# Gathering the experts' tokens with native float32 products from one copy of h

## Chip, core and metric

The kernel runs on one core of one Trainium2 chip. The metric is the device time of one execution in microseconds (us), taken as the median of three runs. TensorE (PE in the profile) does all the matrix products; ScalarE (ACT) and VectorE (DVE) empty its accumulators (PSUM) and compute the small things between; GpSimd (POOL) and SyncE (SP) mostly start transfers.

## What is computed

One inference step of a network with four layers over 256 tokens (128 context tokens and 128 latent tokens, width 1024). Each layer mixes the tokens (pooling, attention, Fourier, pooling) and then applies a mixture of 16 experts, of which each token uses two out of one group of four. All data are float32.

```python
def moe(h, router_w, router_b, w_gate, w_up, w_down):
    scores = jax.nn.sigmoid((h @ router_w).astype(jnp.float32))
    ...
    gates = jnp.sum(jax.nn.one_hot(idx, N_EXPERTS, dtype=jnp.float32) * wts[..., None], axis=-2)
    g = jnp.einsum('bnd,edf->bnef', h, w_gate)
    u = jnp.einsum('bnd,edf->bnef', h, w_up)
    a = jax.nn.silu(g) * u * gates[..., None].astype(h.dtype)
    return jnp.einsum('bnef,efd->bnd', a, w_down)
```

The kernel does not compute every expert for every token. It collects the tokens of an expert into 64 slots, computes the expert for these, and adds the result back to the tokens.

## The kernel before

**Order of the work.** Each engine has one hand-written program, and semaphores tie them together. A layer is a mixer, a norm, the router, and then a loop over the four groups of experts (line 1359 on PE, 664 on ACT, 1009 on DVE). With these inputs each group needs one round of 64 slots per expert, so the loop runs 4 times per layer and 16 times in all.

**Weights.** All weights come through one ring of 12 slots of 1 MiB (`ring`), loaded by SP in the order in which PE uses them. SP starts the load of a unit as soon as PE has used the unit 12 places before it (`s_used`), and PE waits for a unit in `unit` (line 1039). One pass of the expert loop uses 24 units. Behind the experts of layer 0 come 8 units of `ada_w` (used in two halves, with the norm between), then the units of `attn_wqkv`, of which the first product (line 1145) needs two at once. Behind the experts of layer 2 come 8 units of `ada_w` and then one of `pool_w` (line 1099).

**Loads by POOL.** At the first norm of layer 1 POOL starts the loads of `braw` (a table of many short rows), `kattn`, `ck` and `cv` (lines 462 to 465). They are released by `s_ms`, which DVE raises in line 707, so they follow the end of the experts of layer 0.

**The router.** PE computes the logits (line 1282), then turns h so that tokens are on the partitions (`by_token`, line 1289, four pieces of 128x512). ACT copies each piece into `h_hi` with rounding to float32r (`high`, line 634), and DVE writes what the rounding left off into `h_lo` (`low`, line 887). Pieces 2 and 3 reuse the banks of 0 and 1, so PE waits for `s_tlo` before them (line 1298). Meanwhile DVE ranks the experts (lines 893 to 927); its `s_mask` releases PE's counting products (lines 1309 to 1313), but PE first goes through the copies of x into the accumulators (line 1305). From the counts DVE makes the positions (lines 942 to 952) and the first `onehot` (line 997), and this releases the first gather.

**The gather.** It is a matrix product too: h, with tokens on the partitions, is the stationary operand (128x128), and the matrix `onehot` (token to slot, four experts side by side, 256 columns) streams past it. There are 8 blocks of channels and 2 sequences, and each product is done for `h_hi` and for `h_lo`: 32 products of 128x128 by 256 columns in each pass of the loop. ACT copies each pair of blocks from PSUM to `xg` (line 669). Later in the pass DVE makes the next `onehot` (line 997).

**The rest of a pass.** Gate and up projections (lines 1388 and 1390, which run side by side in the two halves of the array), the turn of their result (line 1412), the down projection (line 1425), and the combination (line 1435).

Of the kernel before, what the change touches and what calls it, by code (L numbers as in the profile page):

```python
# [156 lines left out]
def build(nc, x_prompt, x_sample, cache_k, cache_v, c, c_ctx, ada_w, ada_b, norm1_g, norm2_g, pool_w,  # L157
# [4 lines left out]
    with ctx:  # L162
# [57 lines left out]
        with ExitStack() as moe:  # L220
            hT = sb("hT", [P, DB, T], F32, moe)
            junk = sb("junk", [P, NSEQ * D], F32, moe)
            tmp = sb("tmp", [P, 512], F32, moe)
            h_hi = sb("h_hi", [P, NSEQ, D], F32R, moe)
            h_lo = sb("h_lo", [P, NSEQ, D], F32R, moe)
            xg = sb("xg", [P, DB, GROUP, SLOTS], F32, moe)
            onehot = sb("onehot", [P, NSEQ, GROUP, P], F32R, moe)
            gated = sb("gated", [P, NSEQ, GROUP, P], F32, moe)
            gatedT = sb("gatedT", [P, GROUP, T], F32, moe)
            gu = sb("gu", [P, FB, P], F32, moe)  # L230
            sg = sb("sg", [P, FB, SLOTS], F32, moe)
            act = sb("act", [P, FB, SLOTS], F32, moe)
# [96 lines left out]
        s_sig = sem("s_sig")  # L329
        s_tok = sem("s_tok")  # L330
        s_thi = sem("s_thi")
        s_tlo = sem("s_tlo")
        s_mask = sem("s_mask")
        s_pos = sem("s_pos")
        s_posx = sem("s_posx")
# [156 lines left out]
        def _(ac):  # L492
# [133 lines left out]
            def router(l):  # L626
                ac.wait_ge(s_lg, l + 1)
                nc.scalar.activation(r_sc[:, :, :], ps[:, B_Y, 0:2 * E].rearrange("p (s e) -> p s e", s=NSEQ),
                                     ACT.Sigmoid).then_inc(s_sig, 1)

                def high(i):
                    ac.wait_ge(s_tok, 4 * l + i + 1)
                    m = (i % 2) * 64
                    nc.scalar.activation(h_hi[:, i // 2, :].rearrange("p (b m) -> p b m", b=DB)[:, :, m:m + 64],
                                         ps[:, i % 2, :].rearrange("p (m b) -> p b m", b=DB), ACT.Copy).then_inc(s_thi, 1)

                high(0)
                high(1)
                for s in range(NSEQ):
                    ac.wait_ge(s_bc2, 2 * l + s + 1)  # L640
                    nc.scalar.activation(g2x[:, s, :], ps[:, B_ACC + s, :], ACT.Copy).then_inc(s_g2x, 1)
                high(2)
                high(3)
# [42 lines left out]
        def _(v):  # L686
# [192 lines left out]
                ada_mods(9)  # L879
                projected(l, "four", 2, (6, 7, 4, 5))  # L880

            def low(l, i):
                v.wait_ge(s_thi, 4 * l + i + 1)
                m = (i % 2) * 64
                hi = h_hi[:, i // 2, :].rearrange("p (b m) -> p b m", b=DB)[:, :, m:m + 64]
                lo = h_lo[:, i // 2, :].rearrange("p (b m) -> p b m", b=DB)[:, :, m:m + 64]
                v.tensor_tensor(lo, ps[:, i % 2, :].rearrange("p (m b) -> p b m", b=DB), hi.bitcast(F32),
                                ALU.subtract).then_inc(s_tlo, 1)

            def router(l):  # L890
                v.wait_ge(s_sig, l + 1)
                sc = r_sc[:, :, :]
# [23 lines left out]
                    link(v.tensor_tensor(r_ge[:, 0:n, :], r_ge[:, 0:n, :], r_gt[:, 0:n, :], ALU.add))  # L916
                    link(v.tensor_reduce(out, ge, AX_X, ALU.add))

                low(l, 0)
                low(l, 1)  # L920
                best = r_best[:, :]
                rank(best.rearrange("p (s g) -> p s g", s=NSEQ), r_gs[:, :, :], NSEQ)
                link(v.tensor_scalar(best, best, 0.0, None, ALU.is_equal))
# [3 lines left out]
                v.tensor_tensor(mask.rearrange("p s (g e) -> p (s g) e", e=GROUP), r_rank[:, :, :],  # L927
                                best.unsqueeze(2).to_broadcast([P, NSEQ * NG, GROUP]), ALU.mult).then_inc(s_mask, 1)
                v.wait_ge(s_mask, l + 1)
                low(l, 2)  # L930
                low(l, 3)
                link(v.tensor_tensor(r_w[:, :, :], sc, mask, ALU.mult))
                link(v.tensor_reduce(r_den[:, :], r_w[:, :, :], AX_X, ALU.add))
                link(v.reciprocal(r_den[:, :], r_den[:, :]))
# [21 lines left out]
            for l in range(DEPTH):  # L956
                base = bases[l]
                if l == 0:
                    norm_chain(0)
                    ada_rows(0, 0, 0)  # L960
                    ada_mods(0)
                else:
                    out_of_experts(base)
                    norm_chain(2 * l)
                    ada_first = {1: 4, 2: 9, 3: 10}[l]
                modulated(l, 0, 2 * l)
                if l > 0:
                    ada_rows(ada_first, l, base)
                if KINDS[l] == 0:
                    mixer_pool(l)  # L970
                    if l == 0:
                        ada_rows(1, 0, 0)
                        ada_mods(1)
                    else:
                        ada_mods(10)
                    pool_added(l)
                elif KINDS[l] == 1:
                    attention(l)
                else:
                    fourier(l)  # L980
                norm_chain(2 * l + 1)
                if l == 0:
                    ada_rows(2, 0, 0)
                    ada_mods(2)
                if l == 3:
                    ada_rows(11, l, base)
                    ada_mods(11)
                modulated(l, 1, 2 * l + 1)
                router(l)
                if l == 0:  # L990
                    ada_rows(3, 0, 0)
                    ada_mods(3)

                def onehots(group, g, count):
                    pos = posx[:, :, :, :].rearrange("p k s e -> p (k s e)")[:, bass.ds(group * 8, 8)]
                    gate = gx[:, :, :, :].rearrange("p g s e -> p (g s e)")[:, bass.ds(g * 8, 8)]
                    v.tensor_tensor(onehot[:, :, :, :].rearrange("p s e c -> p (s e) c"),  # L997
                                    iota.unsqueeze(1).to_broadcast([P, 8, P]),
                                    pos.unsqueeze(2).to_broadcast([P, 8, P]), ALU.is_equal).then_inc(s_oh, 1)
                    v.wait_ge(s_oh, count)  # L1000
                    v.tensor_tensor(gated[:, :, :, :].rearrange("p s e c -> p (s e) c"),
                                    onehot[:, :, :, :].rearrange("p s e c -> p (s e) c").bitcast(F32),
                                    gate.unsqueeze(2).to_broadcast([P, 8, P]), ALU.mult).then_inc(s_gated, 1)

                v.wait_ge(s_posx, 1)
                onehots(0, 0, base + (l + 1))
                v.wait_ge(s_g2x, 2 * (l + 1))
                n = v.value_load(rounds[0:1, l:l + 1], min_val=1, max_val=MAX_ROUNDS)
                with v.Fori(0, n * NG) as k:
                    it = v.snap(base + k)  # L1010
                    it4 = v.snap(it * 4)
                    g_next = v.snap((k + 1) & (NG - 1))
                    k_next = v.snap(k + 1)
                    v.wait_ge(s_oht, it * 2 + 2)
                    onehots(k_next, g_next, it + (l + 2))
                    for e in range(GROUP):
                        v.wait_ge(s_silu, it4 + (e + 1))
                        v.tensor_tensor(act[:, :, :], sg[:, :, :],  # L1018
                                        ps[:, B_T, :].rearrange("p (j c) -> p j c", c=P)[:, :, SLOTS:2 * SLOTS],
                                        ALU.mult).then_inc(s_prod, 1)  # L1020
                        v.wait_ge(s_used, used(EXPERTS_AT[l] + AT_IN_GROUP[("dn", e, 1)], l, it))
                        for s in range(NSEQ):
                            ins = v.tensor_tensor(ysb[:, e % 2, s, :], ps[:, B_Y, :], g2x[:, s, :], ALU.mult)  # L1023
                        ins.then_inc(s_y, 1)
                bases.append(v.snap(base + n * NG))
# [12 lines left out]
        def _(pe):  # L1038
# [237 lines left out]
            def router(l, base):  # L1276
# [18 lines left out]
                if l == 0:  # L1295
                    ada(3, 0, 4, l, base)
                for i in (2, 3):
                    pe.wait_ge(s_tlo, 4 * l + i - 1)
                    by_token(i)


# [22 lines left out]
            for l in range(DEPTH):  # L1324
# [29 lines left out]
                router(l, base)  # L1354

                pe.wait_ge(s_rounds, l + 1)
                pe.wait_ge(s_tlo, 4 * l + 4)
                n = pe.value_load(rounds[0:1, l:l + 1], min_val=1, max_val=MAX_ROUNDS)
                with pe.Fori(0, n * NG) as k:
                    it = pe.snap(base + k)  # L1360
# [4 lines left out]
                    def gather(j):  # L1365
                        if j >= 2:
                            pe.wait_ge(s_xg, it4 + (j - 1))
                        for d in range(2):
                            b = 2 * j + d
                            n2 = 0  # L1370
                            for h in (h_hi, h_lo):
                                for s in range(NSEQ):
                                    mm = pe.matmul(ps[:, (B_G, B_T)[j % 2], d * 256:(d + 1) * 256], h[:, s, b * P:(b + 1) * P],  # L1373
                                                   onehot[:, s, :, 0:SLOTS], start=(n2 == 0), stop=(n2 == 3))
                                    n2 += 1
                        mm.then_inc(s_ga, 1)

                    def gate_up(e, h):

                        ug, uu = at + AT_IN_GROUP[("gate", e, h)], at + AT_IN_GROUP[("up", e, h)]  # L1380
                        if e > 0 and h == 0:
                            pe.wait_ge(s_guc, it4 + e)
                        wg, wu = unit(ug, l, it), unit(uu, l, it)
                        for i in range(4):
                            b = 4 * h + i
                            if e == 0 and b % 2 == 0:
                                pe.wait_ge(s_xg, it4 + (b // 2 + 1))
                            mg = pe.matmul(ps[0:SLOTS, B_GU, :], xg[:, b, e, :], wg[:, i * F:(i + 1) * F],  # L1388
# [105 lines left out]
```

## Time and profile before

| What | Value |
|---|---|
| Median of 3 runs | 1498.91 us (1497.91 to 1500.8) |
| The profiled execution, its own time | 1498.94 us |
| Its span, first to last instruction | 1497.1 us |
| PE busy | 1369.8 us (91%) |
| DVE busy | 319.0 us (21%) |
| ACT busy | 247.0 us (16%) |
| Read from memory | 532.24 MB, 357 GB/s over the span |
| Mean granted clock of TensorE | 0.953 of full speed |

How to read it: the profile lists each executed matrix product as one or more records. A float32 product, such as line 1145, leaves two records; a float32r product, such as those of line 1373 before the change, leaves one. A record's listed duration includes the time in which it overlaps its neighbours, so what a product costs is read from the distance between starts, or from the length of a run of them divided by their number. Most of the engines other than PE wait most of the time, and their waits cost nothing so long as PE is not waiting for them.

### The profile page before, as it was taken

The numbers are of one execution on the slowest core, as the hardware profiler recorded it, in microseconds if no ns is written. First come the engines' busy times: TensorE is split into PE (matmuls) and PEld (weight loads), VectorE is DVE, ScalarE is ACT, GpSimd is POOL, SyncE is SP. The second block draws the span as 40 slices with busy tenths as digits, with TensorE's granted clock in tenths as the row PEclk, the third lists the DMA queues.
The fourth block names the chain that finished last, engine by engine and source line by source line (L and its number), as shares of the span: only waits on it lengthen the run. The fifth ranks groups of instructions, "written<-read, shape, count | busy, mean of one in ns | idle before, by whom it ended". The sixth has DMA issues, their size and how long they took to land.

```text
span 1497.1 us, 17845 instructions
## 1 busy us (share of the span) xinstructions
PE 1369.8 (91%) x6753; PEld 627.2 (42%) x6753; DVE 319.0 (21%) x719; ACT 247.0 (16%) x528; POOL 38.3 (3%) x75
## 2 busy tenths in 40 slices
PE   4889999996998788999999998999999979999997
PEld 2443434433864445433434355443433445344342
DVE  1232111112012422311111313211111333111112
ACT  2121101101001212201101222211101222011011
POOL 2000000001000100000000000000000000000000
PEclk9989999998998878899999998999999988999999
DMA  9999999999856972399999973499999994999994
GB/s 375 421 417 398 421 422 422 422 422 361 327 206 272 381 294 112 122 422 422 422 421 421 415 290 113 182 422 422 421 422 422 415 421 158 412 422 422 422 422 189
DMA packets 86958, 535.00 MB, mean 357 GB/s; under 512 B 11160, under 2 KB 13304, under 8 KB 25472
## 3 DMA queue, kind: packets, MB, share of 16 engines
q1 hardware_dynamic: 82048, 527.47, 86.1%
q0 software_dynamic: 3120, 5.23, 1.1%
q10 hardware_dynamic: 1744, 1.71, 0.3%
q8 instruction: 27, 0.44, 0.1%
q14 instruction: 19, 0.16, 0.0%
HBM read 532.24 MB, written 2.12 MB: 357 GB/s over the span
## 4 chain that ended last, share of the span: by engine, by line
PE 87%; DMA 6%; DVE 4%; ACT 3%; issue 1%; SPq 0%; DVEq 0%; ACTq 0%
PE ps L1388 30%; PE ps L1425 14%; PE ps L1435 7%; PE ps L1373 5%; PE ps L1050 4%; PE ps L1145 4%; PE ps L1121 4%; PE ps L1412 2%; DMA ring<-in_attn_wqkv_dram 2%; PE ps L1069 2%; PE ps L1158 2%; DMA ring<-in_pool_w_dram 2%; DMA ring<-in_ada_w_dram 2%; PE ps L1282 1%; PE ps L1305 1%; PE ps L1401 1%
## 5 line engine op out<-in xcount | busy, mean ns | idle before, releaser
L1388 PE MATMUL ps<-ring,xg 128*64 128x512 f32 x1024 | 466.1, 598 | 11.6 <-ACT gu L677 11.6
L1390 PE MATMUL ps<-ring,xg 128*64 128x512 f32 x1024 | 466.0, 598 | 0.0
L1388 PEld LDWEIGHTS ps<-ring,xg 128*64 128x64 f32 x1024 | 131.1, 137 | 279.0 <-issue 251.2
L1425 PE MATMUL ps<-ring,act 128*64 128x512 f32 x1024 | 231.4, 594 | 0.0
L1023 DVE TENSOR_TENSOR gb<-ps,g2x 128x512 f32<-128x512 f32 x128 | 82.5, 686 | 368.7 <-PE ps L1425 368.7
L1425 PEld LDWEIGHTS ps<-ring,act 128*64 128x64 f32 x1024 | 72.1, 137 | 149.2 <-issue 137.0
L1390 PEld LDWEIGHTS ps<-ring,xg 128*64 128x64 f32 x1024 | 131.2, 137 | 0.0
L1435 PE MATMUL ps<-gb,gatedT 64*128 64x512 f32 x512 | 122.9, 609 | 0.0
L1050 PE MATMUL ps<-ring,cact 128*32 128x512 f32 x768 | 96.2, 648 | 17.2 <-ACT cact L505 5.7
L680 ACT ACTIVATE sg<-ps 128x256 f32<-128x256 f32 x64 | 24.5, 383 | 374.9 <-PE ps L1412 374.9
L1018 DVE TENSOR_TENSOR act<-sg,ps 128x256 f32<-128x256 f32 x64 | 26.8, 418 | 231.9 <-ACT sg L680 231.9
L1435 PEld LDWEIGHTS ps<-gb,gatedT 64*128 64x128 f32 x512 | 45.4, 186 | 66.4 <-issue 61.5
L677 ACT ACTIVATE gu<-ps 128x512 f32<-128x512 f32 x64 | 38.2, 597 | 202.9 <-PE ps L1390 202.9
L1145 PE MATMUL ps<-hT,ring 128*128 128x256 f32 x256 | 58.7, 393 | 11.2 <-DMA ring<-in_attn_wqkv_dram 11.2
L1373 PE MATMUL ps<-onehot,h_hi 128*128 128x256 f32 x256 | 55.9, 302 | 10.3 <-DVE onehot L997 10.3
L1069 PE MATMUL ps<-diag,x 128*128 128x128 f32 x256 | 40.0, 330 | 25.2 <-DVE diag L715 25.2
L669 ACT ACTIVATE xg<-ps 128x512 f32<-128x512 f32 x64 | 38.3, 598 | 146.8 <-PE ps L1373 146.8
L997 DVE TENSOR_TENSOR onehot<-const,posx 128x1024 fp32r<-128x1024 f32 x20 | 24.5, 1225 | 168.1 <-PE ps L1401 168.0
L1145 PEld LDWEIGHTS ps<-hT,ring 128*128 128x128 f32 x256 | 50.4, 198 | 20.0 <-issue 12.9
L1050 PEld LDWEIGHTS ps<-ring,cact 128*32 128x32 f32 x768 | 24.0, 118 | 78.4 <-issue 57.5
L1373 PE MATMUL ps<-onehot,h_lo 128*128 128x256 f32 x256 | 53.9, 294 | 0.0
L1069 PEld LDWEIGHTS ps<-diag,x 128*128 128x128 f32 x256 | 38.8, 244 | 31.4 <-DVE diag L715 23.6
(183 smaller groups left out, 1027.0 us busy)
## 6 DMA issues: line engine op xcount, KB each, us to landing
ring<-in_moe_w_gate_dram SPq DMA_DIRECT2D x128, 1024.0 KB, 13.9
ring<-in_moe_w_up_dram SPq DMA_DIRECT2D x128, 1024.0 KB, 15.8
ring<-in_moe_w_down_dram SPq DMA_DIRECT2D x128, 1024.0 KB, 14.5
ring<-in_ada_w_dram SPq DMA_DIRECT2D x96, 1024.0 KB, 18.5
ring<-in_attn_wqkv_dram SPq DMA_DIRECT2D x12, 1024.0 KB, 14.7
ring<-in_attn_wo_dram SPq DMA_DIRECT2D x4, 1024.0 KB, 13.4
ring<-in_fourier_w_dram SPq DMA_DIRECT2D x4, 1024.0 KB, 23.7
ring<-in_pool_w_dram SPq DMA_DIRECT2D x2, 1024.0 KB, 26.3
```

The costliest lines, as they stand in the source:

```text
L669: nc.scalar.activation(xg[:, 2 * j:2 * j + 2, :, :].rearrange("p b e s -> p (b e s)"), ps[:, (B_G, B_T)[j % 2], :], ACT.Copy).then_inc(s_x ...
L677: nc.scalar.activation(gu[:, :, :], ps[:, B_GU, :].rearrange("p (m j) -> p j m", j=FB), ACT.Copy).then_inc(s_guc, 1)
L1023: ins = v.tensor_tensor(ysb[:, e % 2, s, :], ps[:, B_Y, :], g2x[:, s, :], ALU.mult)
L1050: mm = pe.matmul(ps[32 * j:32 * (j + 1), B_ADA, :], cact[:, i, :], w[:, j * 512:(j + 1) * 512], start=(i == 0), stop=(i == ADA_UNITS - 1))
L1069: mm = pe.matmul(ps[:, B_ACC + j, at:at + SEQ], x[:, s, b * P:(b + 1) * P], diag[:, s, :], start=True, stop=True)
L1121: mm = pe.matmul(ps[:, banks[2 * cc + s], :], src[:, 4 * h + b, s * SEQ:(s + 1) * SEQ], w[:, b * 512:(b + 1) * 512], start=(h == 0 and b = ...
L1145: mm = pe.matmul(ps[:, job_bank(i + n), d * T:(d + 1) * T], w[b // 4][:, at:at + P], hT[:, b, :], start=(b == 0), stop=(b == DB - 1))
L1373: mm = pe.matmul(ps[:, (B_G, B_T)[j % 2], d * 256:(d + 1) * 256], h[:, s, b * P:(b + 1) * P], onehot[:, s, :, 0:SLOTS], start=(n2 == 0), s ...
L1388: mg = pe.matmul(ps[0:SLOTS, B_GU, :], xg[:, b, e, :], wg[:, i * F:(i + 1) * F], start=(b == 0), stop=(b == DB - 1))
L1390: mu = pe.matmul(ps[SLOTS:P, B_GU, :], xg[:, b, e, :], wu[:, i * F:(i + 1) * F], start=(b == 0), stop=(b == DB - 1))
L1425: mm = pe.matmul(ps[r * SLOTS:(r + 1) * SLOTS, B_Y, :], act[:, j, :], w[:, i * D + r * HALF:i * D + (r + 1) * HALF], start=(j == 0), stop= ...
L1435: mm = pe.matmul(ps[:, B_ACC + 2 * s + r, :], gatedT[part, e, s * SEQ:(s + 1) * SEQ], ysb[part, e % 2, s, :], start=False, stop=False, ski ...
```

## The change

The rounded part and the remainder are replaced by one float32 copy of h, `onehot` becomes float32, and the gather does one float32 product where it did two float32r products. DVE's `low` and its semaphore `s_tlo` go, and what waited for `s_tlo` waits for ACT's `s_thi` instead. In `gate_up` a parameter is renamed, since `h` now names the tile.

```diff
-            h_hi = sb("h_hi", [P, NSEQ, D], F32R, moe)
-            h_lo = sb("h_lo", [P, NSEQ, D], F32R, moe)
+            h = sb("h", [P, NSEQ, D], F32, moe)
...
-            onehot = sb("onehot", [P, NSEQ, GROUP, P], F32R, moe)
+            onehot = sb("onehot", [P, NSEQ, GROUP, P], F32, moe)
...
-                    nc.scalar.activation(h_hi[:, i // 2, :].rearrange("p (b m) -> p b m", b=DB)[:, :, m:m + 64],
+                    nc.scalar.activation(h[:, i // 2, :].rearrange("p (b m) -> p b m", b=DB)[:, :, m:m + 64],
...
-            def low(l, i):
-                v.wait_ge(s_thi, 4 * l + i + 1)
...
-                v.tensor_tensor(lo, ps[:, i % 2, :].rearrange("p (m b) -> p b m", b=DB), hi.bitcast(F32),
-                                ALU.subtract).then_inc(s_tlo, 1)
...
-                low(l, 0)
-                low(l, 1)
...
-                low(l, 2)
-                low(l, 3)
...
                 for i in (2, 3):
-                    pe.wait_ge(s_tlo, 4 * l + i - 1)
+                    pe.wait_ge(s_thi, 4 * l + i - 1)
                     by_token(i)
...
-                pe.wait_ge(s_tlo, 4 * l + 4)
+                pe.wait_ge(s_thi, 4 * l + 4)
...
-                            n2 = 0
-                            for h in (h_hi, h_lo):
-                                for s in range(NSEQ):
-                                    mm = pe.matmul(ps[:, (B_G, B_T)[j % 2], d * 256:(d + 1) * 256], h[:, s, b * P:(b + 1) * P],
-                                                   onehot[:, s, :, 0:SLOTS], start=(n2 == 0), stop=(n2 == 3))
-                                    n2 += 1
+                            for s in range(NSEQ):
+                                mm = pe.matmul(ps[:, (B_G, B_T)[j % 2], d * 256:(d + 1) * 256], h[:, s, b * P:(b + 1) * P],
+                                               onehot[:, s, :, 0:SLOTS], start=(s == 0), stop=(s == 1))
```

## Rows read from the trace of the kernel before

**Rows 1.** The page: busy time, its share of the span, instructions.

```profile
PE 1369.8 (91%) x6753; PEld 627.2 (42%) x6753; DVE 319.0 (21%) x719; ACT 247.0 (16%) x528; POOL 38.3 (3%) x75
```

**Rows 2.** The chain that ended last: start us, length us, what.

```profile
171.86 4.01 PE ps L1373 x32
...
229.91 4.01 PE ps L1373 x32
...
336.32 33.49 DMA ring<-in_attn_wqkv_dram
369.95 16.80 PE ps L1145 x64
...
387.19 13.82 PE ps L1145 x64
```

**Rows 3.** Timeline of PE around the gather at 288 us: start us, length us.

```profile
287.89 0.50 PE L1373 MATMUL ps<-onehot,h_hi 128*128 128x256 f32 x2
...
291.57 0.40 PE L1373 MATMUL ps<-onehot,h_lo 128*128 128x256 f32 x2
291.89 0.64 PE L1388 MATMUL ps<-ring,xg 128*64 128x512 f32 x1
```

**Rows 4.** Groups of instructions: count, busy us, mean ns, idle before and its releaser.

```profile
L669 ACT ACTIVATE xg<-ps 128x512 f32<-128x512 f32 x64 | 38.3, 598 | 146.8 <-PE ps L1373 146.8
L997 DVE TENSOR_TENSOR onehot<-const,posx 128x1024 fp32r<-128x1024 f32 x20 | 24.5, 1225 | 168.1 <-PE ps L1401 168.0
L887 DVE TENSOR_TENSOR h_lo<-ps,h_hi 128x512 fp32r<-128x512 f32 x16 | 11.0, 691 | 10.3 <-ACT h_hi L634 9.7
```

**Rows 5.** Timeline of the router of layer 1, PE and DVE.

```profile
602.82 1.97 PE L1289 MATMUL ps<-const,hT 128*128 128x128 f32 x8
...
603.67 0.19 DVE L927 TENSOR_TENSOR r_mask<-r_rank,r_best 128x32 f32<-128x32 f32 x1
604.58 5.12 PE L1305 MATMUL ps<-x,const 128*128 128x512 f32 x8
...
610.83 0.19 DVE L942 SCALAR_TENSOR_TENSOR r_pm<-ps,r_mask 128x32 f32<-128x32 f32 x1 [3.75 <-PE ps L1313]
```

**Rows 6.** Stages: length, PE busy, then granted clock, DMA share, GB/s.

```profile
287.90:346.00 58.10, 57.38 (x286) 22.37 (x288) 9.19 (x14) 7.40 (x14) 0.00 (x0) 1.00 1.01 422
346.00:355.00 9.00, 7.23 (x65) 4.52 (x64) 5.50 (x18) 5.93 (x15) 4.95 (x7) 1.00 1.02 383
355.00:370.00 15.00, 3.77 (x35) 1.01 (x33) 2.48 (x6) 0.80 (x3) 2.08 (x4) 0.73 1.04 302
370.00:380.00 10.00, 10.00 (x34) 8.38 (x35) 0.00 (x0) 0.12 (x1) 0.00 (x0) 0.72 1.05 386
```

**Rows 7.** Loads issued in 140:200, in 260:300, in 333:337: median us to landing.

```profile
ring<-in_moe_w_gate_dram SPq DMA_DIRECT2D x8, 1024.0 KB, 12.5
...
ring<-in_moe_w_gate_dram SPq DMA_DIRECT2D x6, 1024.0 KB, 16.9
...
ring<-in_ada_w_dram SPq DMA_DIRECT2D x2, 1024.0 KB, 20.9
```

**Rows 8.** All waits of PE for a load of the ring: total us, times, longest.

```profile
PE ps L1145 <- DMA ring<-in_attn_wqkv_dram: 11.2, 1, 11.2
PE ps L1050 <- DMA ring<-in_ada_w_dram: 1.7, 1, 1.7
PE ps L1099 <- DMA ring<-in_pool_w_dram: 1.1, 1, 1.1
```

**Rows 9.** Timeline between the experts of layer 0 and the qkv products.

```profile
345.94 3.64 PE L1050 MATMUL ps<-ring,cact 128*32 128x512 f32 x32
...
349.37 3.32 POOL L462 DMA_DIRECT2D braw<-bias_rows  x4 [235.62 <-DVE ms L707]
...
355.08 3.64 PE L1050 MATMUL ps<-ring,cact 128*32 128x512 f32 x32
355.19 1.37 DVE L740 TENSOR_SCALAR hT<-ps,amul,mods 128x128 f32<-128x128 f32 x4 [0.35 <-PE ps L1069]
```

More of the change, by code:

```diff
@@ L331, in build @@
         s_thi = sem("s_thi")
-        s_tlo = sem("s_tlo")
         s_mask = sem("s_mask")
@@ L880, in fourier @@
                 projected(l, "four", 2, (6, 7, 4, 5))
-            def low(l, i):
-                v.wait_ge(s_thi, 4 * l + i + 1)
-                m = (i % 2) * 64
-                hi = h_hi[:, i // 2, :].rearrange("p (b m) -> p b m", b=DB)[:, :, m:m + 64]
-                lo = h_lo[:, i // 2, :].rearrange("p (b m) -> p b m", b=DB)[:, :, m:m + 64]
-                v.tensor_tensor(lo, ps[:, i % 2, :].rearrange("p (m b) -> p b m", b=DB), hi.bitcast(F32),
-                                ALU.subtract).then_inc(s_tlo, 1)
             def router(l):
@@ L1001, in onehots @@
                     v.tensor_tensor(gated[:, :, :, :].rearrange("p s e c -> p (s e) c"),
-                                    onehot[:, :, :, :].rearrange("p s e c -> p (s e) c").bitcast(F32),
+                                    onehot[:, :, :, :].rearrange("p s e c -> p (s e) c"),
                                     gate.unsqueeze(2).to_broadcast([P, 8, P]), ALU.mult).then_inc(s_gated, 1)
@@ L1369, in gather, with gate_up @@
                             b = 2 * j + d
-                            n2 = 0
-                            for h in (h_hi, h_lo):
-                                for s in range(NSEQ):
-                                    mm = pe.matmul(ps[:, (B_G, B_T)[j % 2], d * 256:(d + 1) * 256], h[:, s, b * P:(b + 1) * P],
-                                                   onehot[:, s, :, 0:SLOTS], start=(n2 == 0), stop=(n2 == 3))
-                                    n2 += 1
+                            for s in range(NSEQ):
+                                mm = pe.matmul(ps[:, (B_G, B_T)[j % 2], d * 256:(d + 1) * 256], h[:, s, b * P:(b + 1) * P],
+                                               onehot[:, s, :, 0:SLOTS], start=(s == 0), stop=(s == 1))
                         mm.then_inc(s_ga, 1)
-                    def gate_up(e, h):
-                        ug, uu = at + AT_IN_GROUP[("gate", e, h)], at + AT_IN_GROUP[("up", e, h)]
-                        if e > 0 and h == 0:
+                    def gate_up(e, half):
+                        ug, uu = at + AT_IN_GROUP[("gate", e, half)], at + AT_IN_GROUP[("up", e, half)]
+                        if e > 0 and half == 0:
                             pe.wait_ge(s_guc, it4 + e)
@@ L1384, in gate_up @@
                         for i in range(4):
-                            b = 4 * h + i
+                            b = 4 * half + i
                             if e == 0 and b % 2 == 0:
```

## The prediction

> **What bounds the kernel now.** I began with the page. PE is busy for 91% of the span, every other engine for a fifth or less [rows 1], so the first question about any edit is what it does to PE. The chain of work that ended last says the same in detail: inside the expert loop it never leaves PE, and each gather stands in it with 4.01 us, 58.05 us after the one before (229.91 - 171.86) [rows 2]. Anything added to PE in a pass therefore lengthens the pass, until something else gets slower than PE.
>
> The only thing near that is the stream of weights. In the expert passes of layer 0 the transfer engines are full (share 1.01) and move 422 GB/s [rows 6]. A pass uses 24 units of 1,048,576 bytes, 25.17 MB, which takes 59.6 us at that rate, while PE gets through a pass in 58.05 us. So the loads fall behind PE by 1.6 us in each pass. One sees it in how long a load takes from issue to landing: 12.5 us in the second pass, 16.9 us in the fourth, 20.9 us at its end [rows 7]. The debt is paid behind the experts of layer 0: PE waits 11.2 us for the first attn_wqkv units [rows 8], and the chain leaves PE there for a DMA piece from 336.32 to 369.8 [rows 2]. In this stretch and the one behind it the granted clock is 0.73 and 0.72 [rows 6], that is partly the level of 1.2 GHz and partly that of 2.4 GHz: its first 64 records of line 1145 take 16.80 us, the next 64 take 13.82 us [rows 2]. Behind the experts of layer 2 a smaller wait of 1.1 us for pool_w has the same cause [rows 8]. The 1.7 us wait for ada_w lies ahead of the first expert pass and has nothing to do with it.
>
> **What is removed from the gather.** Between the first and the last row of the gather at 288 us, 30 records start in 291.57 - 287.89 = 3.68 us, and the next line starts 0.32 us after the last pair: 4.00 us in all for 32 rounded products, in which a rounded product of 256 columns takes about 0.12 us [rows 3].
>
> **What is added to it.** 16 native products of the same shape (128x128 stationary, 256 columns). Line 1145 is exactly that. One call of `by_channel` makes 2 x 2 outputs from 8 blocks, 32 products, and the chain shows 64 records for it, so one native product leaves two records. At full clock 64 records take 13.82 us, 0.216 us for a record and 0.432 us for a product [rows 2]. So the count of records of a gather stays at 32, but each takes 0.216 us in place of 0.12 us: 32 x 0.216 = 6.91 us, and about 0.14 us at the two joints, of which the 4.00 us hold some 0.2. The gather goes from 4.00 to about 7.05 us, or 3.05 us more. Sixteen passes: **+48.8 us** on PE. From both sides: without the joints 2.9 us (46), with the 0.262 us per record of the slow first 64 [rows 2] for all passes 4.4 us (70). I take 3.05, because the row has the same operands and clock as the passes of the loop (granted clock 1.00 [rows 6]).
>
> ACT's copies to xg take 0.60 us for each two blocks, and PE now takes 1.73 us for them, so ACT stays ahead [rows 4]. Making onehot in float32 is the same DVE work, 1.23 us and in the shade of PE except once in a layer [rows 4]; I cost it at nothing.
>
> **What is removed from DVE.** The 16 subtractions, 0.69 us each, 11.0 us in all [rows 4]. Two of them stand before the ranking that ends in the mask, two after it. They are covered: the mask is ready at 603.86, but PE, which needs it, is in the copies of x (line 1305) until 609.7, since its own order comes first; and DVE then waits 3.75 us for PE's counts (line 942) [rows 5]. Without that cover the subtractions would be worth up to 2.8 us in a layer. PE's wait before the third piece of by_token now falls a subtraction earlier, but PE comes to it only at 602.8, with the gates in between [rows 5], so nothing is won there. **0 us.** Half the room for h in the tile memory changes no time.
>
> **What is given back.** With 61.1 us a pass PE is slower than the stream's 59.6 us, and the loads no longer fall behind. So the debt is not there to be paid. Layer 0: PE leaves the experts 12.2 us later. In the kernel before it was free for the qkv products at 355.08 + 3.64 = 358.7 [rows 9], now at 370.9. When do their two units land? The last ada_w loads were issued by 333 to 337 and landed some 20.9 us later, about 354.2. They are issued 12.2 us later now, but the three passes' debt of 3 x 1.6 = 4.8 us is gone, so they land at about 361.6. Two units more take 5.5 us at 383 GB/s [rows 6]: 367. POOL's loads of 2.2 MB start at 349.37 + 12.2 = 361.6 [rows 9] and share the engines; at worst all their 5.2 us come first: 372. So the wait shrinks from 11.2 us to between 0 and 1 us; I take 0: **-11.2 us**. The Trainium skill bears on the worst case: its page "Trainium Kernel Development and Optimization", Key Constraints, says that transfers started from SP, ACT and POOL run on the same 16 engines and interleave. The fall to 302 GB/s while POOL's loads run [rows 6] agrees. By that rule the qkv units would come about 5 us later than alone, and the sum would be 1 us higher.
>
> Without the idle time PE should also keep its full clock into line 1145, as it has it at 346 to 355 [rows 6]: 16.80 - 13.82 = **-3.0 us** [rows 2]. The page "TensorE: Matmul & The Clock Gate", Part 1, says the same of idle and busy stretches; the 0.73 after the wait agrees. Layer 2: the 1.1 us wait for pool_w goes: **-1.1 us** [rows 8]. Layers 1 and 3 have no such wait behind their experts, the last one only the end; nothing is given back there.
>
> **The sum.** 48.8 - 11.2 - 3.0 - 1.1 = **+33.5 us**. By layer: 0 gives -2.0, 1 gives 12.2, 2 gives 11.1, 3 gives 12.2. The profiled execution took 1498.94 us, practically the median of 1498.91, and its span of 1497.1 lies 1.8 inside. The prediction is 1498.9 + 33.5 = **1532.4 us**, 2.2% slower.
>
> **Rivals.**
> *The debt stays.* The loads are released by PE's use of the ring, so a slower PE also issues them later; if the stream loses as much as PE, the wait of 11.2 us, the slow clock and the pool wait stay: +48.8, 1547.7 us. For it: the load of the unit waited for is issued by PE's progress (336.32) and takes 33.5 us [rows 2], and POOL's loads move along with PE. Against: most of those 33.5 us are queue, and the queue grew only because a pass was shorter than its 59.6 us. Chance 0.12 for this or half of it.
> *The native product is cheap.* This would end on the other side. If one native product of 256 columns cost as much as a single rounded one, a gather would lose 16 x 0.12 us: 16 passes give -30.7 us, 1468 us. It decides from 0.24 us per product, the price of the two rounded ones that it replaces: below it the kernel is faster, at it equal. Line 1145 shows 0.43 us [rows 2], and I know no reason why the gather's operands should be treated otherwise. Chance 0.03. The page "FP8 and Floating Point Precision", TensorE Precision Notes, gives a true float32 product four passes of the array; that would be the upper price, and line 1145 agrees with it.
> *Equal.* The native product costs just what two rounded ones do, 0.24 us, and the 16 subtractions stay hidden: 1499 us. Same evidence against it. Chance 0.04.
> *The clock falls more often.* A different rhythm of the stages between the passes, or the longer gather, puts more of PE's work at 1.2 GHz. If all gathers ran at the 0.262 us of the slow records, the sum is 70 - 15 = +55, 1554 us. Chance 0.06 for this or a part that leaves the main range.
>
> **The numbers.** The main case has the other 0.75, with its own range of 1527 to 1538. For 8 in 10 the range goes from 1525 (every gather at the low bound and some slow clock saved elsewhere) to 1548 (the debt stays). A measurement of this kernel tells about 0.2%, 3 us, from no change. Faster has 0.03, same 0.04, slower 0.93.
>
> **What would show it.** Line 1373 should have 512 records as before, but starting 0.216 us apart, with 7.0 us for a gather in the chain, and the expert passes should be 61.1 us apart. Their transfer rate should fall from 422 to about 412 GB/s (25.17 MB in 61.1 us), and the share a little below 1. The wait of line 1145 for attn_wqkv should be gone or under 1 us, and the granted clock behind it near 1. DVE's wait before line 942 should grow by the 1.4 us of two subtractions, and PE's start of the first gather of a layer should not move against its router. The prediction is wrong if the distance of the native records is not that of line 1145, or if the wait of 11.2 us is still there behind the longer passes.

## The result, and the profile after

The changed kernel takes **1538.59 us** (median of 4 runs, 1536.73 to 1540.06) against 1499.09 us: a ratio of 1.0262 with a 95% interval of 1.0244 to 1.028, 39.5 us slower. A second series (`after_again`, below) gave 1537.23 us and 1.025 (1.0236 to 1.0264). The forecast was 1532.4 us, with a range of 1525 to 1548. The profiled execution took 1536.73 us, with a span of 1534.9 us. Lines 1131, 1357, 1371, 1408, 1036 and 983 of the changed kernel are lines 1145, 1373, 1388, 1425, 1050 and 997 of the one before. In the kernels of the experiments the line numbers differ by up to a dozen.

The page, and the groups that answer to [rows 1] and [rows 4]:

```profile
PE 1419.4 (92%) x6753; PEld 661.0 (43%) x6753; DVE 308.9 (20%) x703; ACT 247.1 (16%) x528; POOL 38.3 (2%) x75
...
L1357 PE MATMUL ps<-onehot,h 128*128 128x256 f32 x512 | 119.8, 394 | 10.3 <-DVE onehot L983 10.3
L667 ACT ACTIVATE xg<-ps 128x512 f32<-128x512 f32 x64 | 38.2, 597 | 196.8 <-PE ps L1357 196.8
L983 DVE TENSOR_TENSOR onehot<-const,posx 128x1024 f32<-128x1024 f32 x20 | 24.5, 1225 | 218.1 <-PE ps L1384 218.0
```

PE has the same 6753 records, of which the gather has 512 as before, and DVE has 16 instructions less. ACT's wait for the gather grew by 50.0 us (146.8 in [rows 4], 196.8 here): that is the added length of the 16 gathers, seen from the engine that waits for them. The making of onehot did not change.

The chain that ended last, beside [rows 2]:

```profile
177.34 7.10 PE ps L1357 x32
...
238.49 7.10 PE ps L1357 x32
...
351.09 22.54 DMA ring<-in_attn_wqkv_dram
373.76 14.05 PE ps L1131 x64
388.25 13.81 PE ps L1131 x64
```

A gather holds 7.10 us of the chain (4.01 before), and the passes are 61.15 us apart (58.05 before). The DMA piece is still there in front of the qkv products, but it is 22.5 us long and not 33.5, and the first 64 records behind it take 14.05 us and not 16.80. The timeline of PE around one gather, beside [rows 3]:

```profile
299.56 7.17 PE L1357 MATMUL ps<-onehot,h 128*128 128x256 f32 x32
306.67 0.64 PE L1371 MATMUL ps<-ring,xg 128*64 128x512 f32 x1
```

It takes 306.67 - 299.56 = 7.11 us to the next line; 4.00 us before.

What became of the waits for loads (compare [rows 8]), and of the rate in the passes (the second is the stage before the qkv products; columns as in [rows 6]):

```profile
PE ps L1036 <- DMA ring<-in_ada_w_dram: 2.2, 2, 1.7
...
PE ps L1131 <- DMA ring<-in_attn_wqkv_dram: 0.3, 1, 0.3
```

```profile
238.50:299.60 61.10, 60.38 (x281) 24.39 (x281) 9.20 (x14) 7.40 (x14) 0.00 (x0) 1.00 1.00 413
...
367.50:373.80 6.30, 6.02 (x55) 3.23 (x53) 2.98 (x9) 2.86 (x8) 1.60 (x3) 1.00 1.06 256
```

The wait of 11.2 us is down to 0.3, the wait for pool_w is gone, and the stream runs at 413 GB/s in a pass, which is what PE now asks for. The last ada_w loads of the layer (issued in 344:350) land 15.7 us after issue, not 20.9 us [rows 7]:

```profile
ring<-in_ada_w_dram SPq DMA_DIRECT2D x3, 1024.0 KB, 15.7
```

**Where the time went.** The start of DVE's onehot instruction marks the passes, so the span can be cut there. The pieces add up to the span; a second profile of the same kernel stands beside the first.

| Piece, us | before | after | difference | after_again | difference |
|---|---|---|---|---|---|
| start to first onehot | 112.48 | 114.86 | +2.4 | 112.68 | +0.2 |
| four passes of layer 0 | 184.26 | 196.65 | +12.4 | 196.65 | +12.4 |
| from there to layer 1's first onehot | 315.57 | 300.81 | -14.8 | 303.29 | -12.3 |
| four passes of layer 1 | 185.78 | 198.25 | +12.5 | 198.34 | +12.6 |
| to layer 2's | 145.84 | 145.93 | +0.1 | 147.60 | +1.8 |
| four passes of layer 2 | 185.79 | 198.34 | +12.6 | 198.15 | +12.4 |
| to layer 3's | 121.93 | 121.94 | 0.0 | 121.63 | -0.3 |
| four passes of layer 3 | 185.68 | 198.34 | +12.7 | 198.34 | +12.7 |
| the rest (the last pass and the end) | 59.77 | 59.78 | 0.0 | 59.8 | 0.0 |

The onehot of a pass is made inside the pass before it, behind that pass's gather. So each row "four passes" holds the four gathers of its layer, and the end of the fourth pass stands in the row below it. The gathers cost 50.0 us, and the piece with the qkv products gives back 12 to 15.

The start wanders by up to 2.4 us, but the +1.8 us behind layer 1 are more than wandering. That piece took 145.8 to 145.9 us in the profiles of `before`, `no_remainder`, `pool_late` and `braw_late`, 145.93 us in the first profile of the changed kernel, and 147.6 us in the three others with the full native gather (`after_again`, `after_pool_late`, `native_and_subtraction`). No wait of PE differs there between `before` and `after_again`; what differs is the granted clock from 120 to 130 us after the layer's last onehot, 0.83 before and 0.73 in `after_again`:

```profile
918.09:928.09 10.00, 8.03 (x57) 7.87 (x57) 3.10 (x10) 4.29 (x9) 0.00 (x0) 0.83 0.32 134
```

```profile
930.96:940.96 10.00, 8.02 (x47) 7.86 (x47) 3.11 (x10) 4.29 (x9) 0.00 (x0) 0.73 0.32 133
```

What sets the clock there in one execution and not in another, no run shows.

### The profile page after: what moved, and what is told of

Same layout as the page of the kernel before. It is cut to its first block, busy times and chain, and to the rows that moved or that the text cites. A ratio compares the mean times of both kernels' runs of the same rounds, so it can differ in the third digit from the quotient of the medians.

```text
span 1534.9 us, 17821 instructions
## 1 busy us (share of the span) xinstructions
PE 1419.4 (92%) x6753; PEld 661.0 (43%) x6753; DVE 308.9 (20%) x703; ACT 247.1 (16%) x528; POOL 38.3 (2%) x75
## 4 chain that ended last, share of the span: by engine, by line
PE 89%; DVE 4%; DMA 3%; ACT 3%; issue 1%; SPq 0%; DVEq 0%; ACTq 0%
PE ps L1371 29%; PE ps L1408 14%; PE ps L1357 8%; PE ps L1418 7%; PE ps L1036 4%; PE ps L1131 4%; PE ps L1107 4%; PE ps L1395 2%; PE ps L1055 2%; PE ps L1144 2%; DMA ring<-in_ada_w_dram 2%; PE ps L1268 2%; DMA ring<-in_attn_wqkv_dram 1%; PE ps L1291 1%; PE ps L1384 1%; PE ps L1069 1%
## 5 line engine op out<-in xcount | busy, mean ns | idle before, releaser
L1357 PE MATMUL ps<-onehot,h 128*128 128x256 f32 x512 | 119.8, 394 | 10.3 <-DVE onehot L983 10.3
L1357 PEld LDWEIGHTS ps<-onehot,h 128*128 128x128 f32 x512 | 99.4, 197 | 33.8 <-DVE onehot L983 10.8
L1036 PE MATMUL ps<-ring,cact 128*32 128x512 f32 x768 | 97.2, 653 | 17.4 <-ACT cact L503 5.4
L678 ACT ACTIVATE sg<-ps 128x256 f32<-128x256 f32 x64 | 24.6, 384 | 374.8 <-PE ps L1395 374.8
L1418 PEld LDWEIGHTS ps<-gb,gatedT 64*128 64x128 f32 x512 | 45.4, 186 | 66.4 <-issue 61.6
L667 ACT ACTIVATE xg<-ps 128x512 f32<-128x512 f32 x64 | 38.2, 597 | 196.8 <-PE ps L1357 196.8
L983 DVE TENSOR_TENSOR onehot<-const,posx 128x1024 f32<-128x1024 f32 x20 | 24.5, 1225 | 218.1 <-PE ps L1384 218.0
## 6 DMA issues: line engine op xcount, KB each, us to landing
ring<-in_moe_w_gate_dram SPq DMA_DIRECT2D x128, 1024.0 KB, 12.4
```

What stands on the lines that cost most here:

```text
L667: nc.scalar.activation(xg[:, 2 * j:2 * j + 2, :, :].rearrange("p b e s -> p (b e s)"), ps[:, (B_G, B_T)[j % 2], :], ACT.Copy).then_inc(s_x ...
L1036: mm = pe.matmul(ps[32 * j:32 * (j + 1), B_ADA, :], cact[:, i, :], w[:, j * 512:(j + 1) * 512], start=(i == 0), stop=(i == ADA_UNITS - 1))
L1418: mm = pe.matmul(ps[:, B_ACC + 2 * s + r, :], gatedT[part, e, s * SEQ:(s + 1) * SEQ], ysb[part, e % 2, s, :], start=False, stop=False, ski ...
```

## Experiments

All ratios are to runs of the kernel before in the same series.

**The subtractions alone** (`no_remainder`). The DVE half of the change without the PE half.

```diff
-                low(l, 0)
-                low(l, 1)
...
-                low(l, 2)
-                low(l, 3)
...
-                            for h in (h_hi, h_lo):
+                            for h in (h_hi, h_hi):
```

> The kernel before, in which DVE's subtractions are left out and the gather takes the rounded part twice (h_hi, h_hi), so the remainder of h is missing from the result. PE has the same 32 products in a gather. If the subtractions were hidden, as I hold, the time is that of before, 1499 us within 3 us, and DVE's wait before line 942 grows by about 1.4 us. If they stood on the path, it would be up to 11 us shorter, 1488 us.

Measured: 1499.02 us, ratio 0.9994 (0.9984 to 1.0004). The router of layer 1 in the timeline, beside [rows 5]:

```profile
602.25 0.19 DVE L917 TENSOR_TENSOR r_mask<-r_rank,r_best 128x32 f32<-128x32 f32 x1
...
611.27 0.19 DVE L930 SCALAR_TENSOR_TENSOR r_pm<-ps,r_mask 128x32 f32<-128x32 f32 x1 [7.77 <-PE ps L1301]
```

The mask is ready earlier, and DVE turns all of that into a longer wait for PE's counts, 7.77 us against 3.75. The removal is worth nothing. I had written that the wait would grow by 1.4 us, and it grew by 4.0 us: the two subtractions before the mask and the two behind it all lie ahead of this wait (4 x 0.69 = 2.8 us), and their waits for ACT's copies go with them.

**The native products with the subtractions kept** (`native_and_subtraction`). The other half alone: the changed kernel with `low` and its waits.

```diff
+                low(l, 0)
+                low(l, 1)
...
-                    pe.wait_ge(s_thi, 4 * l + i - 1)
+                    pe.wait_ge(s_tlo, 4 * l + i - 1)
```

> The changed kernel with DVE's 16 subtractions and their waits kept (the remainder is written and used by nothing). If they were hidden, it takes what the changed kernel takes, 1538.6 us within 3 us; if their removal had been worth something on the path, it is up to 11 us slower than the changed one.

Measured: 1537.08 us, ratio 1.0238 (1.0214 to 1.0263), the time of the changed kernel. Its waits for the stream are those of the changed kernel too (0.7 us for attn_wqkv). All of the slowdown is in the native products. In its profile the first gather of layer 0 fell into a stretch of low clock (granted clock 0.50 in the middle of it) and took 10.1 us instead of 7.1.

**Half the blocks native** (`half_native`).

```diff
+                            if d == 1:
+                                for s in range(NSEQ):
+                                    mm = pe.matmul(ps[:, (B_G, B_T)[j % 2], 256:512], h_hi[:, s, b * P:(b + 1) * P].bitcast(F32),
+                                                   onehot[:, s, :, 0:SLOTS].bitcast(F32), start=(s == 0), stop=(s == 1))
+                                continue
```

> The kernel before, in which every second block of the gather is one native float32 product of the rounded part (the remainder is left out for these blocks) and the others stay two rounded products. A gather has 16 rounded and 16 native records: 1.55 us more in a pass, 24.8 us in all, and a pass of 59.6 us, even with the stream. If the loads just stop falling behind at this length, the attn_wqkv wait goes from 11.2 us to about 5 us and the whole is 18 to 20 us above before, 1518 us. If the give-back goes with the PE time added, it is 17 us; if the cost of native records is not additive (mixing costs), a pass is longer than 59.7 us.

Measured: 1517.2 us, ratio 1.0106 (1.008 to 1.0132), 17.4 us more by the medians. The onehots are 59.58 us apart in every layer (58.05 before), 1.53 us more: half the price of all blocks, 3.09. A native product costs the same amid rounded ones. The wait and the chain behind it:

```profile
PE ps L1145 <- DMA ring<-in_attn_wqkv_dram: 5.6, 1, 5.6
```

```profile
344.01 27.83 DMA ring<-in_attn_wqkv_dram
371.98 16.69 PE ps L1145 x64
389.11 13.82 PE ps L1145 x64
```

The wait is half gone: 5.6 us are left, where I had put about 5 us from the queue's debt. A give-back in proportion to the PE time added, my other case, would have left about as much, and its 17 us are closer to the 17.4 us than my 18 to 20; this run does not tell the two apart. The first 64 records are as slow (16.69 us) as before the change. How long the wait is does not settle that alone: with 3.2 us (`rounded_twice`) and 2.1 us (`after_again`) they take 14.05 us, but with the same 2.1 us in `pool_late` 15.74 us.

**More PE time without native products** (`rounded_twice`).

```diff
-                            for h in (h_hi, h_lo):
+                            for h in (h_hi, h_lo, h_hi, h_lo):
```

> The kernel before with each block's four rounded products made twice (the second group starts the accumulation anew, so the result is the same): 64 records in a gather in place of 32, about 3.8 us more on PE in a pass (61.9 us), with nothing native in it. If the change costs its time as PE time and gets part back from the stream, this gets back the same: 16 x 3.8 = 61 us less the 11.2 us wait, the slow clock of 3 us behind it and the 1.1 us wait, 45 to 47 us in all, 1545 us. If the wait of 11.2 us stayed (the loads fall back with PE), it is 1560 us. If native products have a cost beyond the distance of their records, this kernel lies lower against its added PE time than the changed one.

Measured: 1552.16 us, ratio 1.0362 (1.0338 to 1.0385), 52.4 us more, which lies between my two figures. The onehots are 61.9 us apart: 3.85 us more for 32 more records, 0.120 us for one, 61.6 us in 16 passes. Of this the piece with the qkv products gave back 11.7 us (303.84 against 315.57), in the same way as in the changed kernel:

```profile
PE ps L1145 <- DMA ring<-in_attn_wqkv_dram: 3.2, 1, 3.2
PE ps L1050 <- DMA ring<-in_ada_w_dram: 2.3, 2, 1.6
```

```profile
352.93 25.45 DMA ring<-in_attn_wqkv_dram
...
378.52 14.05 PE ps L1145 x64
```

So the give-back belongs to longer passes as such and not to the kind of product. The whole came out dearer than my 45 to 47 us, since 3.2 us of the wait stayed, the piece to layer 2 took 2.4 us more, and the piece with pool_w gave nothing back (121.92 us against 121.93).

**Less PE time in the gather** (`half_gather`). Only the rounded part is gathered; the remainder is left out.

```diff
-                            for h in (h_hi, h_lo):
+                            for h in (h_hi,):
```

> The kernel before with one rounded product in place of two in the gather (h_hi alone; the remainder is left out). PE loses 16 x 0.12 = 1.9 us in each of 16 passes, 30.7 us in all, and a pass would take 56.1 us on PE. If the stream of weights stands at 59.6 us a pass just behind PE, as I hold, most of that is given back as waits for loads behind and in the passes: the attn_wqkv wait grows from 11.2 us to near 19 us, the pool_w wait from 1.1 us to near 8 us, layer 1 and 3 save, and the whole gains 12 to 18 us (1481 to 1487 us). If PE alone set the time, it would be 1468 us.

Measured: 1501.15 us, ratio 1.0008 (0.9999 to 1.0017). I expected a gain of 12 to 18 us, and there is none. The passes are 56.62 us apart, 1.43 us shorter and not 1.9; about 0.2 us of the missing 0.5 is a wait of PE for ACT's copies inside the gather. That is still 23.8 us less in the passes, and the pieces between the layers took it all back: 321.32, 159.01 and 127.57 us against 315.57, 145.84 and 121.93, 24.6 us in all. The waits of PE:

```profile
PE ps L1050 <- DMA ring<-in_ada_w_dram: 16.8, 12, 4.5
...
PE ps L1145 <- DMA ring<-in_attn_wqkv_dram: 7.1, 1, 7.1
...
PE ps L1373 <- ACT xg L669: 2.7, 13, 0.2
...
PE ps L1388 <- DMA ring<-in_moe_w_up_dram: 2.0, 5, 0.7
PE ps L1099 <- DMA ring<-in_pool_w_dram: 1.4, 1, 1.4
```

Waits for the ring are 27.3 us where they were 14.0, and the short stops now come between the ada_w units, where they drag the clock down. The stages behind the experts of layer 1, this kernel and then the one before:

```profile
843.00:880.00 37.00, 32.78 (x125) 13.72 (x118) 8.34 (x25) 9.70 (x20) 5.65 (x11) 0.82 1.03 409
```

```profile
847.00:880.00 33.00, 30.88 (x155) 14.81 (x154) 10.51 (x29) 11.51 (x24) 5.66 (x11) 1.00 1.03 408
```

The waits for loads grew by 13.3 us, near what I had counted (some 15), but not where I had put them: the attn_wqkv wait is 7.1 us and not near 19. About 12 of the 13.3 us lie between the layers. The other 12 to 13 us are not waits. In the piece behind layer 1, 13.2 us longer, only 3.6 us are waits for loads; its mean granted clock is 0.89 against 0.95 before, and 0.82 against 1.00 in the stretch above. So the lower clock makes up most of the rest there; for the other two pieces I did not separate it. The kernel before thus stands at a bend: PE time taken out of its passes gave nothing here, and of PE time put in 77 to 85% was paid (38.3 and 39.5 of 50.0 us in the change, 52.4 of 61.6 in `rounded_twice`).

**POOL's loads later** (`pool_late`).

```diff
             pool.wait_ge(s_bias, 32)
+            pool.wait_ge(s_job, 1)
```

> The kernel before, in which POOL starts its loads of braw, kattn, ck and cv (2.2 MB) only when the first job of the qkv products is done (s_job 1), behind the load that PE waits for. If these loads share the engines with the attn_wqkv units, the wait of 11.2 us shrinks by about 5 us and the kernel takes 1494 us. If the wait is all the weights' own queue, nothing changes; if the late loads are then missed at line 1172, it gets slower.

Measured: 1488.7 us, ratio 0.9926 (0.9914 to 0.9939), 11 us faster than before and the fastest kernel of the study.

```profile
PE ps L1146 <- DMA ring<-in_attn_wqkv_dram: 2.1, 1, 2.1
```

```profile
336.21 24.32 DMA ring<-in_attn_wqkv_dram
360.53 0.14 issue
360.67 15.74 PE ps L1146 x64
```

The load that PE waits for is issued at the same time as before (336.21, 336.32 before) and lands 9.2 us sooner, so POOL's 2.2 MB had cost it 9.2 us, and not the 5.2 us that their bytes take at 422 GB/s. The wait fell from 11.2 to 2.1 us, and the first 64 records got 1.1 us back.

In the profiles with such a wait (save `half_gather`, where PE also stops for ada_w on the way), PE comes to the qkv products 22.2 to 22.3 us after the load was issued (33.5 - 11.2 before, 22.5 - 0.3 in the changed kernel, 24.3 - 2.1 here). So the wait is the time of this load less 22.3 us.

**Only braw later** (`braw_late`).

```diff
+            (kattn, ck and cv are loaded first, where braw was)
+            pool.wait_ge(s_job, 1)
             for r in range(2):
                 for kr in range(2):
```

> The kernel before, in which POOL loads kattn, ck and cv (1.1 MB) where it did, but braw (1 MB in four loads of short rows) only behind the first qkv job. pool_late gained 11 us where I had foreseen 5, so the 2.2 MB cost more than their bytes at 422 GB/s. If the short rows of braw are the dear part, this gains 7 to 10 us (1490 to 1493 us); if every byte of POOL's loads costs the same, it gains half, 5 us (1494.5 us).

Measured: 1492.66 us, ratio 0.9958 (0.9945 to 0.9972), 6.3 us faster; the wait is 4.9 us and the load lands after 27.09 us.

```profile
336.75 27.09 DMA ring<-in_attn_wqkv_dram
363.98 16.62 PE ps L1146 x64
```

So braw's 1.05 MB cost 6.4 us of the 9.2 (33.49 - 27.09), and the 1.18 MB of kattn, ck and cv 2.8 us, which is what their bytes take at 422 GB/s. The dear load is braw, at 164 GB/s. The rates say the same. From 355 to 360 us the transfer engines are full in both kernels, but they move 212 GB/s before, with braw's loads under way, and 396 GB/s in this kernel, with kattn, ck and cv alone:

```profile
355.00:360.00 5.00, 3.72 (x34) 0.94 (x32) 2.48 (x6) 0.80 (x3) 0.23 (x1) 1.00 1.05 212
```

```profile
355.00:360.00 5.00, 4.07 (x37) 1.24 (x35) 2.38 (x7) 1.15 (x4) 0.00 (x0) 1.00 1.04 396
```

Braw's rows are short (64 float32 values, 256 bytes), and that is my reading of the price. But its neighbouring rows also start only one value apart in memory, and no run separates this from the length.

**Both together** (`after_pool_late`). The changed kernel with the same later POOL loads.

```diff
             pool.wait_ge(s_bias, 32)
+            pool.wait_ge(s_job, 1)
```

> The changed kernel, with POOL's loads of braw, kattn, ck and cv started behind the first qkv job as in pool_late. The wait that this shortens is only 0.3 us in the changed kernel, so if the 11 us that pool_late gained were that wait and the slow clock behind it, nothing is to be had here: 1536 to 1539 us. Against pool_late (1488.7 us) the change then costs its full PE time, 48 to 50 us. If POOL's loads cost the changed kernel something beside that wait, it gets 5 us or more faster.

Measured: 1534.59 us, ratio 1.0238 (1.0213 to 1.0262). Against the changed kernel's 1538.59 and 1537.23 us that is 2.6 to 4.0 us; the runs of the three overlap (up to 1540.02 us here, from 1534.19 us in `after_again`), so no gain is shown, as I had foreseen for an attn_wqkv wait of 0.3 us, and it is far from the 11 us that the same edit brought to the kernel before. The span of its profile is 3.3 us below that of the changed kernel, but 3.75 us of difference lie before the first onehot (111.11 against 114.86). The load for which PE waits in the other kernels (here issued between 346 and 350 us) takes 18.8 us and lands before PE asks for it:

```profile
ring<-in_attn_wqkv_dram SPq DMA_DIRECT2D x1, 1024.0 KB, 18.8
```

So in the changed kernel POOL's loads cost this load 3.7 us (22.5 - 18.8) to 5.6 us (24.4 in `after_again`), where they cost it 9.2 us before. Against `pool_late` the change costs 45.9 us, not the 48 to 50 I expected: PE's four gathers a layer cost the same 50 us, and the piece behind layer 0 still gives back 5.3 us (300.03 against 305.35), which are the 2.1 us wait, 1.7 us of slow records (15.74 against 14.01) and 1.5 us that stay open.

**The changed kernel once more** (`after_again`). No edit.

> The changed kernel unaltered, once more. Its profile began the first gather 2.4 us later than the kernel before, although the program is the same up to the router of layer 0, and after_pool_late began it 3.8 us earlier than that. If this is the spread of single executions, the first onehot starts anywhere between 111 and 115 us again, and the time is 1536 to 1540 us; if it belongs to the changed kernel, the first onehot starts at 114 to 115 us again.

Measured: 1537.23 us (1534.19 to 1538.96), first onehot at 112.68 us. The same program up to there gave 114.86 and 111.11 us in the other two profiles. The granted clock from 20 to 60 us was 0.96, 0.91 and 1.00 in these three, in this order:

```profile
20.00:60.00 40.00, 35.25 (x210) 18.38 (x202) 8.21 (x24) 8.93 (x18) 4.38 (x9) 0.96 1.03 409
```

```profile
20.00:60.00 40.00, 34.65 (x207) 18.61 (x200) 8.20 (x24) 7.88 (x16) 3.68 (x8) 0.91 1.03 408
```

```profile
20.00:60.00 40.00, 34.93 (x216) 16.89 (x212) 8.21 (x24) 9.99 (x20) 4.37 (x9) 1.00 1.03 408
```

So the 2.4 us are of the size by which single executions differ, and not shown to be part of the change.

## Why the prediction was right, point by point

The direction and the mechanism were right; the size was 33.5 us where 39.5 us were timed (38.3 in the second series) and 37.8 us stand between the two first spans. The time lies inside the stated range, but at or just above the top of the main case's 1527 to 1538 us.

- **The native products.** Foreseen 3.05 us a pass and 48.8 us, from the distance of line 1145's records; measured 3.09 us and 50.0 us. `half_native` gives half of it, and `native_and_subtraction` and `no_remainder` show that the other half of the change neither costs nor gains anything. Of the 1.2 us between them 0.6 us is the 0.04 us a pass. The other 0.6 us come from the first gathers of the layers (3.1 to 3.4 us more each), three of which ran partly at the slower clock, which I had not counted.
- **The subtractions.** Foreseen and measured as nothing. The step that was wrong is the 1.4 us by which DVE's wait should grow: all four subtractions lie ahead of it, not two. In `no_remainder` it grew by 4.0 us; in the changed kernel by 3.08 us, from 3.75 to 6.83, because the logits came about 1 us later in that execution (DVE's ranking starts at 598.69 us, 597.71 before, and PE's counts end at the same time). It cost nothing.
- **The loads no longer fall behind.** Foreseen 4.8 us of debt gone in layer 0; the last ada_w loads land 5.2 us sooner after issue. Without POOL's loads in the way, the attn_wqkv load takes 24.3 us in `pool_late` and 18.8 us in `after_pool_late`: 5.5 us less, which is the debt by itself. `half_native` loses half of the wait, which the debt explains but does not prove, and `half_gather` shows the other side, where the debt grows.
- **The wait for attn_wqkv.** Foreseen 0 to 1 us left, measured 0.3, 2.1 and 0.7 us in three profiles of kernels with the full native gather, so the bound was a little too tight. The load is issued by PE's progress, so its landing has to be counted from the issue: my 367 to 372 us are 18.5 us without and 23.5 us with POOL's loads behind an issue at 348.5 us (336.32 + 12.2). Measured are 18.8 us without them, and 22.5, 24.4 and 23.0 us with them. The absolute 373.6 us contain the 2.4 us by which this execution started late. So POOL's 5.2 us at worst came out as 3.7 to 5.6 us. That this fitted was luck in part. By the same terms the load of the kernel before should have landed at 354.2 + 5.5 + 5.2 = 364.9 us, and it landed at 369.8: there POOL's loads cost 9.2 us (`pool_late`), and I did not see it. In both kernels they start 13.05 us after the issue of this load. Before the change 11.3 us of it were then still to come even without them, after it 5.8 us, so in the changed kernel they share the engines with it for less time. Of the 9 to 11 us by which the load got faster, 5.5 us are thus the debt and the rest is the smaller cost of POOL's loads, which my account did not have.
- **The clock behind the wait.** Foreseen -3.0 us; the first 64 records took 14.05 us in place of 16.80, so 2.75 us.
- **The wait for pool_w.** Foreseen -1.1 us. The wait did vanish, but the piece to layer 3 took 121.94 us as before (121.93). Behind it, the stretch from the second norm (line 1055, 1069 before) to the first gather took 37.63 us in place of 36.45, with products of the router at a slower clock. The piece was 121.6 us in the three other profiles with the full native gather, so 0.0 to 0.3 us came back and not 1.1.
- **What was not in the sum.** The pieces of `after_again` add up to 39.4 us against the 33.5 of the forecast, and its table column says where the 5.9 us are: 1.2 in the gathers; 1.9 in layer 0, where 12.3 us came back and not 14.2, since 2.1 us of the wait stayed; 1.8 behind layer 1, which I had put at nothing and where the clock fell further; 0.8 at pool_w; 0.2 before the first gather. In the first profile the balance is another (more given back in layer 0, nothing lost behind layer 1, 2.4 us lost at the start) and ends at 37.8 us. So the terms mis-sized are the give-back in layer 0 and two places of slow clock between the layers; why the clock falls there in one execution and not in another stays open.

Of the rivals, a cheap or equal native product is refuted by the distance of its records. That the debt stays is refuted by the waits and by the 1548 us that it would have taken. More slow clock is true in part: about 0.6 us in the first gathers, 1.8 us behind layer 1 in three of four profiles, and what ate the gain of pool_w.

## What to carry to other kernels

Before costing PE work, find out on which side of the transfer stream a pass stands. Here it stood 1.6 us short of it: taking 24 us from the passes gained nothing, adding 50 us cost 38 to 40. A product's price is best read from the distance between records of the same shape and type elsewhere in the trace, counting how many records each product leaves. And when a chain waits for a long load, look for what else was started beside it: one wait added in POOL's program, found by pricing this change, was worth 11 us. Run the terms of a forecast over the kernel before as well: there mine missed the landing of this load by 4.9 us.

## What the runs showed of the hardware that I had not expected

- Braw's transfers (256-byte rows, starting 4 bytes apart) took 6.4 us from the stream for 1.05 MB, 164 GB/s, where kattn, ck and cv cost no more than their bytes at 422 GB/s. From 379 to 384 us of `braw_late`, with braw's loads under way, the full engines moved 214 GB/s.
- POOL's loads beside the stream cost the load that PE waits for 9.2 us when it still had 11.3 us to go, and 3.7 to 5.6 us when it had 5.8 us to go.
- Stops between matrix products can cost more through the clock than through the idle time: behind layer 1 of `half_gather` the waits for loads grew by 3.6 us and the piece by 13.2 us, with a mean granted clock of 0.89 against 0.95.
- The same program up to the first gather took 111.1 to 114.9 us to its first onehot in different executions, with a granted clock of 1.00 to 0.91 in the stretch before.
